# Attention of a hybrid block on one core: scores and meta values from stacked high and low rows, in another order

## The chip, the core and the metric

The kernel runs on one core of a Trainium2 chip. Its engines run side by side and meet at semaphores: PE (TensorE, matmuls into PSUM; PEld is its loading of weights), DVE (VectorE), ACT (ScalarE), POOL (GpSimd) and SP, which issues transfers. The metric is the device time of one execution in microseconds (us), as the median of the runs. Times inside the kernel are from one execution that the hardware profiler took; they count from the start of its span.

## The reference, cut to what matters

One decoder block over 16 meta tokens and 512 tokens: an HGRN2 recurrence and a sliding-window attention side by side, merged by sigmoid gates, then a PEER expert layer. The change lies in the attention:

```
s_band = einsum(q, k of the token's block and of the block before) * scale    # masked to a window of 128
s_meta = einsum(q, k of the 16 meta tokens) * scale
p = softmax(concatenate([s_band, s_meta, sink of the head]))
o = einsum(p_band, v) + einsum(p_meta, v of the meta tokens)
```

There are 8 query heads of 64 dimensions, in two groups with one key and value head each (`s` = 0 and 1 in the code), and 4 blocks of 128 tokens. Float32 accuracy is wanted. A product of float32 values is formed either as one float32 matmul, or from parts: a high part rounded to the matmul's short format (`F32R`) and a low part that holds the rest.

## The kernel before, in words

**Stages.** Input projections (to about 130 us), the recurrence with its chunks of 32 tokens (to 181 us), the attention (181 to 275 us), the branch and output projections, the queries and keys of the expert layer, and from 549 us on the dense and gathered products over the experts. The code of each engine is written out by hand in program order, and semaphores tie the engines together. `S["anorm"]` and its like are those semaphores: `wait_ge` stops an engine until the count is reached.

**The attention** has 16 steps (`HEADS`), one for a pair of heads (one of each group) in one block of tokens: step `p` is block `tt = p // 4`, pair `c = p % 4`. For each:
- PE `scores(p)` (L1823, in the first block L1827 and L1829): two float32 matmuls over 64 rows each, one for a group, with the query as weights and the keys `akx` as 272 moving columns (256 of the band, 16 meta; 144 in the first block).
- DVE `logits(p)`: copies the sink into the last column (L1244), scales and masks (L1245), takes the maximum (L1248).
- ACT `exponentials(p)` (L810), twice, with the row sum.
- DVE `normalise(p)`: reciprocal (L1255), two scalings of `atp` (L1257), the meta part into `atpm` (L1258).
- PE `turn(p)` (L1845, L1846): four transposes (two in the first block) and one of the meta part.
- ACT `turned(p)` (L818, L819): copies what was transposed out of PSUM.
- PE `values(p)` (L1859, L1862, L1865): float32 matmuls of 128 columns, in pairs for the two groups: band before, own band, meta.

When a block of tokens is done, ACT takes its high part (`attention_hi`, L823) and DVE the low part (`attention_lo`, L1264).

**What fills PE in between.** `gate_products` (L1709) are 256 matmuls of 512 columns of the gate projection (and 8 ahead of them), dealt out over the 17 rounds of the loop over `i` by `gates_before`: 15 or 16 in a round. Twenty-four of them use one tile of weights. When those are done, ACT copies the result (L768) and makes the high part of the next tile (L706), POOL makes its low part (L555, 128x1024 elements) and scales the gates (L566). A round is, on PE, `scores(i)`, `turn(i - 1)`, the gate products, `values(i - 1)`. DVE and ACT also split the output of the recurrence (`ohg`, L1280 and L840) in four rounds.

**Ahead of it** DVE builds `avm` and `akx` at about 104 us, while PE still projects, and PE transposes twelve groups of values and keys at 131 us (`avmeta` last). In the experts' part `middle_and_low` (L1416) splits gate values into three bf16 parts.

## Time and profile before

| what | us |
|---|---|
| median of 3 runs (1569.6 to 1570.4) | 1569.93 |
| the profiled execution itself | 1569.61 |
| its span | 1567.9 |
| PE busy, whole span | 1561.1 |
| attention, first scores to first branch product (181.18 to 275.35) | 94.17 |
| PE / DVE / ACT / POOL busy, 181.00 to 275.35 | 94.30 / 53.30 / 50.72 / 39.98 |

A busy time counts overlapping instructions once. A matmul's duration runs from its start to the modelled end, while the next one begins before that; how much of PE's time a matmul takes is therefore read from one start to the next, or from the pieces of the chain of waits, which don't overlap. A duration on DVE or ACT that is far longer than that of the same instruction elsewhere has a wait inside it.

### The profile page before, as it was taken

What the parts mean: (1) busy time and instruction counts of PE and PEld (TensorE: products, weight loads), DVE (VectorE), ACT (ScalarE), POOL (GpSimd) and SP (SyncE); (2) the same over time, 40 slices, a digit from 0 to 9 for tenths busy, and PEclk for the clock granted to TensorE, in tenths of its full rate; (3) what the DMA queues carried; (4) which work ended last, traced back from release to release, by engine and by line L of the source; (5) the groups of instructions that cost most, each with busy time, mean ns of one, the idle gap of its engine ahead of it and who ended that gap; (6) DMA issues with size and microseconds to landing.
All of it is one profiled execution on the core that took longest, in us unless ns stands there. A gap on an engine that the chain in (4) does not pass through costs nothing.

```text
span 1567.9 us, 26041 instructions
## 1 busy us (share of the span) xinstructions
PE 1561.1 (100%) x9638; PEld 1385.4 (88%) x9638; DVE 1250.8 (80%) x2495; ACT 688.6 (44%) x1008; POOL 753.8 (48%) x484
## 2 busy tenths in 40 slices
PE   9999999999999999999999999999999999999998
PEld 9987777888889999999999999898989899888887
DVE  5864565745899899999598888787888888888887
ACT  6323355534434367777434333333333333333334
POOL 4674443434557566654165555455545545322220
PEclk9999999999999999999999999999999999999999
DMA  4222122434223479998899998999999989899994
GB/s 164 94 94 68 56 67 68 150 121 146 82 81 124 121 261 304 341 321 277 310 366 358 334 353 332 354 340 346 338 348 339 367 319 351 296 320 322 330 321 148
DMA packets 151731, 385.45 MB, mean 246 GB/s; under 512 B 11872, under 2 KB 61536, under 8 KB 151520
## 3 DMA queue, kind: packets, MB, share of 16 engines
...
## 4 chain that ended last, share of the span: by engine, by line
PE 89%; DVE 10%; DMA 0%; ACT 0%; issue 0%; SPq 0%
PE ps L2146 31%; PE ps L1989 25%; PE ps L1646 6%; PE ps L1709 6%; PE ps L2007 5%; DVE hot_w L1530 3%; PE ps L1895 3%; DVE rows L1469 2%; PE ps L1608 2%; DVE hot_l L1526 1%; DVE hot_l L1531 1%; DVE hot_l L1527 1%; PE ps L1908 1%; PE ps L2132 1%; PE ps L1654 1%; PE ps L2070 1%
## 5 line engine op out<-in xcount | busy, mean ns | idle before, releaser
L1989 PE MATMUL ps<-hThi,uwhi 128*128 128x352 f32 x1024 | 330.1, 326 | 0.0
L1989 PE MATMUL ps<-hTlo,uwhi 128*128 128x352 f32 x1024 | 327.6, 322 | 0.0
L956 ACT ACTIVATE vwhi<-vraw 128x1024 fp32r<-128x1024 f32 x128 | 135.8, 1061 | 407.9 <-PE ps L2146 349.6
L653 POOL DMA_INDIRECT rows<-in_v,gidx x128 | 164.4, 1284 | 249.9 <-DVE acc L1485 233.6
L653 POOL DMA_INDIRECT rows<-in_u,gidx x128 | 189.8, 1483 | 181.1 <-DVE rows L1478 136.2
L1444 DVE TENSOR_TENSOR vwlo<-vraw,vwhi 128x1024 fp32r<-128x1024 f32 x128 | 156.6, 1223 | 114.5 <-ACT vwhi L956 114.2
L910 ACT ACTIVATE uwhi<-uraw 128x1024 fp32r<-128x1024 f32 x127 | 134.4, 1058 | 169.6 <-PE ps L1989 130.8
L1989 PEld LDWEIGHTS ps<-hTlo,uwhi 128*128 128x128 f32 x1024 | 192.6, 188 | 1.6
L1989 PEld LDWEIGHTS ps<-hThi,uwhi 128*128 128x128 f32 x1024 | 192.2, 188 | 1.9 <-issue 0.3
L1989 PE MATMUL ps<-hThi,uwlo 128*128 128x352 f32 x1024 | 183.8, 322 | 0.0
L2146 PE MATMUL ps<-vwhi,awhi 128*128 128x512 f32 x720 | 183.7, 390 | 0.0
L2146 PE MATMUL ps<-vwlo,awhi 128*128 128x512 f32 x720 | 182.7, 389 | 0.0
L2146 PE MATMUL ps<-vwhi,awlo 128*128 128x512 f32 x720 | 182.7, 389 | 0.0
L613 POOL TENSOR_TENSOR uwlo<-uraw,uwhi 128x1024 fp32r<-128x1024 f32 x52 | 125.5, 2414 | 95.4 <-ACT uwhi L910 53.5
L1485 DVE SCALAR_TENSOR_TENSOR acc<-rows,pick_w,acc 128x1024 f32<-128x1024 f32 x128 | 164.4, 1285 | 3.7 <-DMA rows<-in_v,gidx 1.1
L1989 PEld LDWEIGHTS ps<-hThi,uwlo 128*128 128x128 f32 x1024 | 166.7, 188 | 0.0
L2146 PEld LDWEIGHTS ps<-vwlo,awhi 128*128 128x128 f32 x720 | 135.1, 188 | 28.3
L2146 PEld LDWEIGHTS ps<-vwhi,awlo 128*128 128x128 f32 x720 | 135.1, 188 | 28.1
L1478 DVE SCALAR_TENSOR_TENSOR rows<-rows,ynat 128x1024 f32<-128x1024 f32 x128 | 155.0, 1232 | 4.0 <-DMA rows<-in_u,gidx 3.9
L2146 PEld LDWEIGHTS ps<-vwhi,awhi 128*128 128x128 f32 x720 | 134.0, 188 | 25.7
L555 POOL TENSOR_TENSOR wzlo<-raw,wzhi 128x1024 fp32r<-128x1024 f32 x35 | 86.0, 2457 | 121.7 <-ACT wzhi L706 121.7
L551 POOL TENSOR_TENSOR wlo<-raw,whi 128x1024 fp32r<-128x1024 f32 x28 | 67.2, 2401 | 88.0 <-ACT whi L704 88.0
...
## 6 DMA issues: line engine op xcount, KB each, us to landing
vraw<-in_v SPq DMA_DIRECT2D x128, 512.0 KB, 5.2
...
rows<-in_u,gidx POOLq DMA_INDIRECT x128, 7.4
```

The source lines that it names most:

```text
L555: pool.tensor_tensor(spaced(k, "lo"), loaded(k), spaced(k, "hi").bitcast(F32), ALU.subtract).then_inc(S["w_lo"], 1)
L613: pool.tensor_tensor(u_weights("lo", n, False), uraw[:, n % 2, :], u_weights("hi", n, False).bitcast(F32), ALU.subtract).then_inc(S["u_lo" ...
L653: pool.indirect_dma_start(out=rows[n % SLOTS][:], out_offset=None, in_=u if q < P else v, in_offset=bass.IndirectOffsetOnAxis(ap=gidx[:, q ...
L910: act.activation(u_weights("hi", n, n >= LAG), u_raw(n, k), ACT.Copy).then_inc(S["u_hi"], 1)
L956: act.activation(vw["hi"][:, m % 2, :], vraw[:, m % 2, :], ACT.Copy).then_inc(S["v_hi"], 1)
L1444: dve.tensor_tensor(vw["lo"][:, m % 2, :], vraw[:, m % 2, :], vw["hi"][:, m % 2, :].bitcast(F32), ALU.subtract).then_inc(S["v_lo"], 1)
L1478: dve.scalar_tensor_tensor(out=row[:], in0=row[:], scalar=1.0, in1=ynat[:, 0, :], op0=ALU.mult, op1=ALU.mult, accum_out=dots[:, k:k + 1]). ...
L1485: dve.scalar_tensor_tensor(out=acc[:, 0, :], in0=row[:], scalar=pick_w[:, k:k + 1], in1=acc[:, 0, :], op0=ALU.mult, op1=ALU.add).then_inc( ...
L1646: ins = pe.matmul(dst, z_weights(k, a, c), y[b][:, SLOT[c], own], start=i == 0, stop=i == 3 * DC - 1)
L1709: ins = pe.matmul(ps[:, 2 + t % 2, :], z_weights(t % 2, a, c), y[b][:, SLOT[c], META:LEN], start=i % (3 * DC) == 0, stop=(i + 1) % (3 * DC ...
L1989: ins = pe.matmul(ps[:, k, 0:UCOLS], u_weights(a, k, far)[:, c * P:(c + 1) * P], hT[b][:, c, P + EXTRA:TOK], start=i == 0, stop=i == len(U ...
L2146: ins = pe.matmul(ps[:, 2 + j, :], act_w[a][:, k, j // 2 * P:(j // 2 + 1) * P], vw[b][:, k, j % 2 * 512:(j % 2 + 1) * 512], start=first an ...
```

## The change

Names: `CUR` is 144, a block of keys with the 16 meta keys in front of it.

- **Scores.** The keys are split once into `key_hi` and `key_lo`, each stacked twice in the 128 partitions (64 dimensions, and the same again). The queries of a block are split into `query`, with the high part in 64 partitions and the low part in the other 64. A head's scores are then two matmuls over 128 rows, against the high and the low keys, in the short format. `queries(tt, s)` is new work for DVE: block 0 in the chunk loop, the others in rounds 1, 2, 4, 6, 8 and 10.
- **Order on PE.** `scores(i + 1)` stands in the middle of round `i`'s gate products, `turn(i - 1)` ahead of them; the last `turn_outputs` also moves between gate products.
- **Meta values.** `avmeta` and `atpTm` hold high and low rows in all combinations (4 x 32 rows). ACT writes the high rows of `atpTm` twice, DVE the low rows (`meta_lo`, new). `turn(p)` now also waits for `meta_lo(p - 1)`.
- **Values** are formed for four pairs at once, in 512 columns, once in each block of tokens, in rounds 4, 8, 12 and 16.
- **Sinks** are copied once for all pairs, since `atsc` now has four places.
- **ACT** does `exponentials(i)` ahead of `turned(i - 1)`, DVE `normalise(i)` ahead of `attention_lo`.
- `middle_and_low` has one operation fewer, POOL two memsets fewer.

```diff
+CUR = P + META
+KEY_ROW = (TOK // P) * CUR
...
+QUERIES = {1: (1, 0), 2: (1, 1), 4: (2, 0), 6: (2, 1), 8: (3, 0), 10: (3, 1)}
...
+def low_count(p):
+
+    return min(2 * p + 3, 2 * HEADS)
...
-        avmeta = at("avmeta", [P, P], F32, X + 30144)
-        akx = at("akx", [P, TT - 1, KEYS], F32, X + 22784)
+        avmeta = at("avmeta", [P, P], F32R, X + 30144)
+        avm4 = at("avm4", [P, 2, 2, 2 * META], F32R, X + 30656)
+        key_hi = at("key_hi", [P, 2, KEY_ROW], F32R, Y_END + HH * LEN * 4)
+        key_lo = [at("key_lo0", [P, KEY_ROW], F32R, Y_END + HH * LEN * 4 + 8 * KEY_ROW),
+                  at("key_lo1", [P, KEY_ROW], F32R, X + 22784)]
+        query = at("query", [P, 2, 2, 4, P], F32R, Z + Z_META * LEN * 4)
...
-        atsc = at("atsc", [P, 2, KEYS + 8], F32, X)
-        atp = at("atp", [P, 2, KEYS + 8], F32, X + 2240)
-        atpT = at("atpT", [P, 2, BAND], F32, X + 4480)
-        atpTm = at("atpTm", [P, P], F32, X + 30656)
+        atsc = at("atsc", [P, 4, 2, 2 * CUR], F32, X)
+        atp = at("atp", [P, 2, 2 * CUR], F32, X + 64 * CUR)
+        atpT = at("atpT", [P, 4, 2, BAND], F32, X + 80 * CUR)
+        atpTm = at("atpTm", [P, 4, P], F32R, Z + 8 * LEN * 4)
...
-            pool.memset(avmeta[:], 0.0)
-            pool.memset(atpTm[:], 0.0)
...
-                    act.activation(atp[:, s, lo:KEYS + 1], atsc[:, s, lo:KEYS + 1], ACT.Exp, bias=atstat[:, 0, s:s + 1],
+                    act.activation(atp[:, s, lo:KEYS + 1], atsc[:, p % 4, s, lo:KEYS + 1], ACT.Exp, bias=atstat[:, 0, s:s + 1],
...
             def turned(p):
 
                 lo = P if p < 4 else 0
                 act.wait_ge(S["atr_mm"], p + 1)
-                need(act, S["apv_mm"], p)
-                act.activation(atpT[:, :, lo:BAND], ps[:, 4:6, lo:BAND], ACT.Copy).then_inc(S["atr_out"], 1)
-                act.activation(atpTm[0:2 * META, :], ps[0:2 * META, 4, BAND:BAND + P], ACT.Copy).then_inc(S["atr_out"], 1)
+                c = p % 4
+                need(act, S["apv_mm"], p // 4)
+                act.activation(atpT[:, c, :, lo:BAND], ps[:, 4:6, lo:BAND], ACT.Copy).then_inc(S["atr_out"], 1)
+                for at_row in (0, 4 * META):
+                    ins = act.activation(atpTm[at_row:at_row + 2 * META, c, :], ps[0:2 * META, 4, BAND:BAND + P], ACT.Copy)
+                ins.then_inc(S["atr_out"], 1)
...
             for i in range(HEADS + 1):
                 if i >= 5 and i % 4 == 1:
                     attention_hi(i // 4 - 1)
+                if i < HEADS:
+                    exponentials(i)
                 if i:
                     turned(i - 1)
-                if i < HEADS:
-                    exponentials(i)
...
-            ins.then_inc(S["avm_ok"], 1)
-            for i in range(TT - 1):
-                dve.tensor_copy(akx[:, i, 0:BAND], ak_z[:, META + i * P:META + i * P + BAND])
-            dve.tensor_copy(akx[:, :, BAND:KEYS], ak_z[:, 0:META].unsqueeze(1).to_broadcast([P, TT - 1, META])
-                            ).then_inc(S["akx_ok"], 1)
+            chain.done(ins)
+            both = avm[:].unsqueeze(1).to_broadcast([P, 2, 2 * META])
+            chain.done(dve.tensor_copy(avm4[:, 0], both))
+            dve.tensor_tensor(avm4[:, 1], both, avm4[:, 0].bitcast(F32), ALU.subtract).then_inc(S["avm_ok"], 1)
+            tiles = lambda ap: ap.rearrange("p (i x) -> p i x", x=CUR)
+            rows_of = [slice(s * HD, (s + 1) * HD) for s in range(2)]
+            for s, kv in enumerate(rows_of):
+                own = ak_z[kv, META:LEN].rearrange("p (i x) -> p i x", x=P)
+                first = ak_z[kv, 0:META].unsqueeze(1).to_broadcast([HD, TT, META])
+                for rows_ in rows_of:
+                    dve.tensor_copy(tiles(key_hi[rows_, s])[:, :, META:CUR], own)
+                    ins = dve.tensor_copy(tiles(key_hi[rows_, s])[:, :, 0:META], first)
+                chain.done(ins)
+                high = tiles(key_hi[kv, s].bitcast(F32))
+                for rows_ in rows_of:
+                    dve.tensor_tensor(tiles(key_lo[s][rows_])[:, :, META:CUR], own, high[:, :, META:CUR], ALU.subtract)
+                    ins = dve.tensor_tensor(tiles(key_lo[s][rows_])[:, :, 0:META], first, high[:, :, 0:META], ALU.subtract)
+            ins.then_inc(S["qk_ok"], 1)
...
+            def queries(tt, s):
+
+                kv, other = rows_of[s], rows_of[1 - s]
+                raw_q = aq_z[kv, :, tt * P:(tt + 1) * P]
+                chain.done(dve.tensor_copy(query[kv, tt % 2, s], raw_q))
+                dve.tensor_tensor(query[other, tt % 2, s], raw_q, query[kv, tt % 2, s].bitcast(F32), ALU.subtract
+                                  ).then_inc(S["qk_ok"], 1)
...
+                if c == NCH - 2:
+                    dve.wait_ge(S["z_out"], N_Z)
+                    for s in range(2):
+                        queries(0, s)
...
-                dve.tensor_copy(atsc[:, :, KEYS:KEYS + 1], sink[:].rearrange("p (s c) -> p s c", s=2)[:, :, c:c + 1])
-                chain.done(dve.scalar_tensor_tensor(out=atsc[:, :, lo:KEYS], in0=ps[:, 6:8, lo:KEYS], scalar=HD ** -0.5,
+                if p == 0:
+                    dve.tensor_copy(atsc[:, :, :, KEYS], sink[:].rearrange("p (s c) -> p c s", s=2))
+                chain.done(dve.scalar_tensor_tensor(out=atsc[:, c, :, lo:KEYS], in0=ps[:, 6:8, lo:KEYS], scalar=HD ** -0.5,
...
             def normalise(p):
@@ -1254,9 +1293,19 @@
                 dve.wait_ge(S["aexp"], 2 * (p + 1))
                 chain.done(dve.reciprocal(atstat[:, 2, :], atstat[:, 1, :]))
                 for s in range(2):
-                    dve.tensor_scalar(atp[:, s, lo:BAND], atp[:, s, lo:BAND], atstat[:, 2, s:s + 1], None, ALU.mult)
-                dve.tensor_tensor(atpm[:], atp[:, :, BAND:KEYS], atstat[:, 2, :].unsqueeze(2).to_broadcast([P, 2, META]),
+                    own = atp[:, s, :].rearrange("p (b x) -> p b x", x=CUR)[:, lo // P:2, 0:P]
+                    dve.tensor_scalar(own, own, atstat[:, 2, s:s + 1], None, ALU.mult)
+                dve.tensor_tensor(atpm[:], atp[:, :, P:CUR], atstat[:, 2, :].unsqueeze(2).to_broadcast([P, 2, META]),
                                   ALU.mult).then_inc(S["anorm"], 1)
+
+            def meta_lo(p):
+
+                c, rows_m = p % 4, slice(0, 2 * META)
+                dve.wait_ge(S["atr_out"], 2 * (p + 1))
+                for at_row in (2 * META, 6 * META):
+                    ins = dve.tensor_tensor(atpTm[at_row:at_row + 2 * META, c, :], ps[rows_m, 4, BAND:BAND + P],
+                                            atpTm[rows_m, c, :].bitcast(F32), ALU.subtract)
+                ins.then_inc(S["anorm"], 1)
...
+                normalise(i)
+                if i:
+                    meta_lo(i - 1)
                 if i >= 5 and i % 4 == 1:
                     attention_lo(i // 4 - 1)
-
-                normalise(i)
+                if i in QUERIES:
+                    queries(*QUERIES[i])
                 if i >= HD_AT + 1 and (i - HD_AT) % 2 == 1 and i < HD_AT + 1 + 2 * HH:
                     h = (i - HD_AT) // 2
                     dve.wait_ge(S["ohg_hi"], h + 1)
                     dve.tensor_tensor(ohg["lo"][:, h, :], o_hg[:, h, :], ohg["hi"][:, h, :].bitcast(F32),
                                       ALU.subtract).then_inc(S["ohg_ok"], 1)
+            meta_lo(HEADS - 1)
...
-                chain.done(dve.tensor_tensor(rest, rest, tab[:, 1], ALU.subtract))
-                return dve.tensor_copy(tab[:, 2], rest)
+                return dve.tensor_tensor(tab[:, 2], rest, tab[:, 1], ALU.subtract)
...
-                    srcs = [v_z[:, h, 0:META] for h in range(HH)] if n == 10 else [avm[:]]
-                rows = P if n < 9 else META if n < 11 else 2 * META
+                    srcs = ([v_z[:, h, 0:META] for h in range(HH)] if n == 10 else
+                            [avm4[:].rearrange("p a b m -> p (a b m)").bitcast(F32)])
+                rows = META if 9 <= n < 11 else P
...
-                halves = [slice(s * HD, (s + 1) * HD) for s in range(2)]
-                if tt:
-                    for s, kv in enumerate(halves):
-                        ins = pe.matmul(ps[:, 6 + s, 0:KEYS], aq_z[kv, c, tt * P:(tt + 1) * P], akx[kv, tt - 1, :],
-                                        start=True, stop=True)
-                else:
-                    for s, kv in enumerate(halves):
-                        pe.matmul(ps[:, 6 + s, P:BAND], aq_z[kv, c, 0:P], ak_z[kv, META:META + P], start=True, stop=True)
-                    for s, kv in enumerate(halves):
-                        ins = pe.matmul(ps[:, 6 + s, BAND:KEYS], aq_z[kv, c, 0:P], ak_z[kv, 0:META], start=True, stop=True)
+                pe.wait_ge(S["qk_ok"], 1 + 2 * (tt + 1))
+                lo, first = (0, META + (tt - 1) * CUR) if tt else (P, 0)
+                last = first + KEYS - lo
+                for s in range(2):
+                    pe.matmul(ps[:, 6 + s, lo:KEYS], query[:, tt % 2, s, c, :], key_hi[:, s, first:last], start=True, stop=False)
+                    ins = pe.matmul(ps[:, 6 + s, lo:KEYS], query[:, tt % 2, s, c, :], key_lo[s][:, first:last],
+                                    start=False, stop=True)
                 ins.then_inc(S["asc_mm"], 1)
...
-            pe.wait_ge(S["akx_ok"], 1)
             scores(0)
             gate_products(GATES_TURN + TT * GATES_HG, GATES_TURN + TT * GATES_HG + GATES_MID)
-            turn_outputs(TT - 1)
-
...
             def turn(p):
 
-                pe.wait_ge(S["anorm"], p + 1)
+                pe.wait_ge(S["anorm"], low_count(p - 1) if p else 1)
                 need(pe, S["atr_out"], 2 * p)
                 for s in range(2):
                     for q in range(0 if p >= 4 else 1, 2):
-                        pe.transpose(ps[:, 4 + s, q * P:(q + 1) * P], atp[:, s, q * P:(q + 1) * P], ident[:])
...
-            def values(p):
-
-                tt, c = p // 4, p % 4
-                pe.wait_ge(S["atr_out"], 2 * (p + 1))
-                if c == 0:
-                    need(pe, S["oat_ok"], tt - 1)
+            def values(tt):
+
+                pe.wait_ge(S["atr_out"], 8 * (tt + 1))
+                need(pe, S["oat_ok"], tt - 1)
+                if tt == 0:
                     pe.wait_ge(S["ohg_f"], TT)
+                pe.wait_ge(S["anorm"], low_count(4 * tt + 3))
+                pe.matmul(ps[:, tt % 2, :], avmeta[:], atpTm[:].rearrange("p c t -> p (c t)"), start=True, stop=False)
                 heads = [(s, slice(s * HD, (s + 1) * HD)) for s in range(2)]
-                if tt:
+                for block_, own in ((tt - 1, slice(0, P)), (tt, slice(P, BAND))):
+                    if block_ < 0:
+                        continue
                     for s, kv in heads:
-                        pe.matmul(ps[kv, tt % 2, c * P:(c + 1) * P], avnat[:, tt - 1, kv], atpT[:, s, 0:P],
-                                  start=True, stop=False)
-                for s, kv in heads:
-                    pe.matmul(ps[kv, tt % 2, c * P:(c + 1) * P], avnat[:, tt, kv], atpT[:, s, P:BAND],
-                              start=tt == 0, stop=False)
-                for s, kv in heads:
-                    ins = pe.matmul(ps[kv, tt % 2, c * P:(c + 1) * P], avmeta[:, kv], atpTm[:], start=False, stop=True)
+                        ins = pe.matmul(ps[kv, tt % 2, :], avnat[:, block_, kv], atpT[:, :, s, own], start=False, stop=block_ == tt)
                 ins.then_inc(S["apv_mm"], 1)
 
             for i in range(HEADS + 1):
-                if 1 <= i < HEADS:
-                    scores(i)
                 if i:
                     turn(i - 1)
-                gate_products(gates_before(i), gates_before(i + 1))
-                if i:
-                    values(i - 1)
+                first, last = gates_before(i), gates_before(i + 1)
+                gate_products(first, (first + last) // 2)
+                if i == 0:
+                    turn_outputs(TT - 1)
+                if i + 1 < HEADS:
+                    scores(i + 1)
+                gate_products((first + last) // 2, last)
+                if i and i % 4 == 0:
+                    values(i // 4 - 1)
```

PE, rounds 4 and 5 before, from the last gate product of one round to the first of the next (L1709 are the gate products, L1823 the scores, L1845 and L1846 the turn, the others the values):

```order
L1709 MATMUL ps<-yhi,wzhi 128x512
L1862 MATMUL ps<-atpT,avnat 64x128 x2
L1865 MATMUL ps<-atpTm,avmeta 64x128 x2
L1823 MATMUL ps<-akx,zr 128x272 x2
L1845 MATMUL ps<-ident,atp 128x128 x4
L1846 MATMUL ps<-ident,atpm 32x128
L1709 MATMUL ps<-ylo,wzhi 128x512
```

The same place with the change, in the round that has the values of the first block (L1761 are the gate products, L1877 and L1878 the scores, L1903 and L1909 the values, L1892 and L1893 the turn):

```order
L1761 MATMUL ps<-ylo,wzhi 128x512
L1877 MATMUL ps<-key_hi,query 128x272
L1878 MATMUL ps<-key_lo_86,query 128x272
L1877 MATMUL ps<-key_hi,query 128x272
L1878 MATMUL ps<-key_lo_87,query 128x272
L1761 MATMUL ps<-yhi,wzlo 128x512
...
L1761 MATMUL ps<-yhi,wzhi 128x512
L1903 MATMUL ps<-atpTm,avmeta 128x512
L1909 MATMUL ps<-atpT,avnat 64x512 x2
L1892 MATMUL ps<-ident,atp 128x128 x4
L1893 MATMUL ps<-ident,atpm 32x128
```

The scores have moved ahead of half of the gate products, and the values stand in one place for four steps.

DVE before, one step of the attention, in a round with a part of `ohg`:

```order
L1244 COPY atsc<-sink 128x2
L1245 SCALAR_TENSOR_TENSOR atsc<-ps,bandmask 128x2x272
L1248 TENSOR_REDUCE atstat<-atsc 128x2
L1255 RECIPROCAL atstat<-atstat 128x2
L1257 TENSOR_SCALAR atp<-atp,atstat 128x256 x2
L1258 TENSOR_TENSOR atpm<-atp,atstat 128x32
L1280 TENSOR_TENSOR ohglo<-o_hg,ohghi 128x512
```

DVE with the change, round 8, in which the first group's queries of block 3 are split (L1306 is `meta_lo`, L1211 and L1212 `queries`):

```order
L1284 SCALAR_TENSOR_TENSOR atsc<-ps,bandmask 128x2x272
L1287 TENSOR_REDUCE atstat<-atsc 128x2
L1294 RECIPROCAL atstat<-atstat 128x2
L1297 TENSOR_SCALAR atp<-atp,atstat 128x2x128 x2
L1298 TENSOR_TENSOR atpm<-atp,atstat 128x32
L1306 TENSOR_TENSOR atpTm<-ps,atpTm 32x128 x2
L1211 CAST query<-zr 64x512
L1212 TENSOR_TENSOR query<-zr,query 64x512
L1284 SCALAR_TENSOR_TENSOR atsc<-ps,bandmask 128x2x272
```

The copy of the sink is gone, and `meta_lo` and `queries` stand between one step's normalising and the next step's logits.

## Rows read from the trace of the kernel before

**Rows 1.** The page, parts 1 and 4: busy time by engine, shares of the chain

```profile
PE 1561.1 (100%) x9638; PEld 1385.4 (88%) x9638; DVE 1250.8 (80%) x2495; ACT 688.6 (44%) x1008; POOL 753.8 (48%) x484
PE 89%; DVE 10%; DMA 0%; ACT 0%; issue 0%; SPq 0%
```

**Rows 2.** Windows, attention: us, busy by engine, clock, DMA share, GB/s

```profile
181.00:275.35 94.35, 94.30 (x605) 70.58 (x597) 53.30 (x122) 50.72 (x135) 39.98 (x22) 1.00 0.20 62
```

**Rows 3.** Chain of waits in the attention: start us, us, engine, line

```profile
181.18 0.42 PE ps L1827 x4
...
225.23 0.37 PE ps L1859 x4
225.60 0.22 PE ps L1862 x4
...
226.04 0.66 PE ps L1823 x4
...
227.39 3.44 PE ps L1709 x15
...
233.00 3.71 PE ps L1709 x16
...
253.18 1.13 ACT atp L810 x4
...
275.35 43.75 PE ps L1895 x192
```

**Rows 4.** PE timeline, short-format matmuls of 264, 256 and 128 columns: start us, us

```profile
27.92 2.10 PE L1654 MATMUL ps<-yhi,wzlo 128*128 128x264 f32 x16
...
390.69 0.22 PE L2021 MATMUL ps<-keyparts,q2lo 128*128 128x128 f32 x1
...
390.92 0.22 PE L2021 MATMUL ps<-keyparts,q2lo 128*128 128x128 f32 x1
```

**Rows 5.** PE timeline, four transposes among gate products

```profile
178.61 0.60 PE L1789 MATMUL ps<-ident,o_nat 128*128 128x128 f32 x4
178.97 0.48 PE L1709 MATMUL ps<-yhi,wzhi 128*128 128x512 f32 x1
179.28 0.39 PE L1709 MATMUL ps<-ylo,wzhi 128*128 128x512 f32 x1
```

**Rows 6.** DVE timeline, one step: start us, us, [idle before <-releaser]

```profile
249.66 2.10 DVE L1244 COPY atsc<-sink 128x2 f32<-128x2 f32 x1 [1.35 <-PE ps L1823]
251.68 0.71 DVE L1245 SCALAR_TENSOR_TENSOR atsc<-ps,bandmask 128x544 f32<-128x544 f32 x1
252.42 0.72 DVE L1248 TENSOR_REDUCE atstat<-atsc 128x2 f32<-128x546 f32 x1
254.33 0.17 DVE L1255 RECIPROCAL atstat<-atstat 128x2 f32<-128x2 f32 x1 [1.19 <-ACT atp L810]
254.53 0.61 DVE L1257 TENSOR_SCALAR atp<-atp,atstat 128x256 f32<-128x256 f32 x2
255.07 0.18 DVE L1258 TENSOR_TENSOR atpm<-atp,atstat 128x32 f32<-128x32 f32 x1
```

**Rows 7.** POOL timeline beside that step

```profile
249.35 2.39 POOL L555 TENSOR_TENSOR wzlo<-raw,wzhi 128x1024 fp32r<-128x1024 f32 x1 [3.30 <-ACT wzhi L706]
```

**Rows 8.** Groups by line, 181.00 to 275.35: busy us, mean ns, idle before, releaser

```profile
L1244 DVE COPY atsc<-sink 128x2 f32<-128x2 f32 x16 | 13.0, 813 | 19.3 <-PE ps L1823 12.6 <-PE ps L1829 6.4
L566 POOL TENSOR_TENSOR gates<-gates,rstd 128x512 f32 (+1 forms) x11 | 14.3, 1300 | 0.0
L706 ACT ACTIVATE wzhi<-raw 128x1024 fp32r<-128x1024 f32 x10 | 10.5, 1047 | 0.0
L1280 DVE TENSOR_TENSOR ohglo<-o_hg,ohghi 128x512 fp32r<-128x512 f32 x4 | 2.7, 685 | 0.0
```

**Rows 9.** DVE timeline, an operation with two SBUF inputs, before the attention

```profile
99.92 2.90 DVE L1166 TENSOR_TENSOR qi<-zr,ecol 128x512 f32<-128x512 f32 x1
```

**Rows 10.** Waits, 0 to 300 us: engine, line, releaser, us in total, times, longest

```profile
DVE vnat L1183 <- PE ps L1733: 27.1, 2, 26.0
```

**Rows 11.** DVE timeline, end of the recurrence's states

```profile
175.90 1.11 DVE L1221 SCALAR_TENSOR_TENSOR state<-state,ecol,ps 128x128 f32<-128x128 f32 x4
```

11 lines of the change are left out of this document (6 added, 5 removed).

## The prediction

> **What bounds the kernel now.** First the page: PE is busy 1561.1 of 1567.9 us and holds 89% of the chain that ended last, DVE 10% [rows 1]. The change lies in the attention, so next that stretch alone: PE is busy throughout at full clock, DVE for 53.3 and ACT for 50.7 of 94.35 us [rows 2]. The chain of waits goes through PE from 181.18 to the first branch product at 275.35, 94.17 us [rows 3]. So the attention is bound by PE's work, and what PE loses in work is gained as long as nothing else becomes late. A low busy share of DVE and ACT doesn't say that they have time: their steps hang on one another, and the last question is how long one step's ring through them is.
>
> **PE's work before.** Sixteen gate products take 3.71 us of the chain and fifteen 3.44, 0.230 each, so the 264 of this stretch take 60.7. The rest is 94.2 - 60.7 = 33.5. A late round agrees: 227.39 to 233.00 is 5.61, less 3.44, leaves 2.17, of which the scores are 0.66, the first pair of values 0.37 and a further pair 0.22 [rows 3].
>
> **PE's work after, by part.**
> - Scores: four matmuls in the short format over all 128 rows. Sixteen of 264 columns took 2.10 - 0.16 = 1.94 from start to next start, 0.12 each; a 256 and a 128 column one together took 0.23, so a narrow one about 0.11 [rows 4]. With 272 columns I take 0.125, so 0.50 a step where 0.66 stood; with 144 columns 0.115, so 0.46. Above, 0.17 each if every weight load showed (0.23 less half of a narrow one's 0.12). Sum: 12 x 0.50 + 4 x 0.46 = 7.8.
> - Turn: four transposes between gate products take 0.36, and the gate product behind them starts 0.08 late (0.31 where 0.23 is usual) [rows 5]. With a fifth at 0.11: 0.55, and 0.37 in the first block. Sum: 12 x 0.55 + 4 x 0.37 = 8.1.
> - Values: 128 columns of a pair took 0.22, so 512 columns take 0.88, as four before; one pair in the first block, two in the three others, each time with one meta matmul at 0.23 and 0.15 for getting in (0.37 - 0.22) [rows 3]. Sum: 7 x 0.88 + 4 x 0.38 = 7.7. The gain is here: the meta pairs of sixteen steps shrink to four matmuls. Above, 0.19 more for a pair if the wide float32 ones went at the rate of the scores' (0.66 for 272 columns, 1.07 less 0.88 allowing for their fixed part), 1.3 in all.
> - The last turn of the recurrence: 0.44.
>
> Together 24.0. PE saves **9.5 us**, between 6 and 10.5.
>
> **The ring through DVE and ACT.** In program order DVE now does logits, normalise, `meta_lo`, and, in many rounds, something more, before it comes to the next logits; ACT's exponentials stand between the first two. Before, DVE had waited 1.35 for the next scores at this place [rows 6], so nothing hung on its length. Now the ring runs by itself, since the scores come half a round ahead. One turn of it, from [rows 3] and [rows 6]: scaling to the exponentials' start 253.18 - 251.68 = 1.50; exponentials until the reciprocal 1.15; reciprocal and scalings 0.74; `atpm` 0.10 until the next can start; `meta_lo` two small operations. The trace has none of these. Below it is 0.10 each, above half of the 0.71 that 544 columns from PSUM take; I take 0.23, nearer to the 0.18 of the one of 32 columns. Sum **3.95**. It is longer by
> - `queries`, 64x512 copied and subtracted. Two scalings of 256 took 0.54, so 0.46 with its wait for 512; a subtraction of that width takes 0.685 [rows 8] and 0.60 if another follows. I take 1.06; above, 1.35.
> - `ohg`'s low part and `attention_lo`, 0.60 each.
>
> Rounds 4 to 10 hold queries four times, `ohg` three times and `attention_lo` twice: 7 x 3.95 + 4 x 1.06 + 5 x 0.60 = 34.9. PE in those rounds: 7 x (0.50 + 0.55) + 108.5 x 0.230 + 1.26 + 2.14 of values = 35.7. Even without a further wait the two are level.
>
> **The further wait is POOL.** The sink's copy of two elements lasted 2.10, until the end of POOL's 2.39 [rows 6, 7]; the sixteen averaged 0.813 [rows 8] where 0.17 would do. An operation with two SBUF inputs lasted 2.90 in the same way [rows 9] where 0.685 is usual. The sinks' copies are gone and with them about 10 us of such waits, but those lay beside PE's work. What remains takes their place, now inside the ring: the scalings in every round, both operations of `queries`, `ohg`'s low part. POOL holds 2.39 + 1.30 for each 24 gate products, 7.7 us at 5.0 for a round of 15.5: a place that meets it at random waits (2.39 x 2.39 + 1.30 x 1.30) / 2 / 7.7 = 0.48. Rounds 4 to 10 have 7 scalings, 4 queries and 3 `ohg`: 14 x 0.48 = 6.7. The ring is then 41.6, and PE waits **5.9**.
>
> Outside those rounds: the first scalings stand behind the recurrence's last turn, which is moved to later, and behind POOL, while PE comes to `turn(0)` sooner, 0.5. Rounds 1 to 3 have a ring of 3.1 and 4.1 with queries against PE's 4.4, about even, 0.2. Rounds 11 to 14 have a ring of 3.95 + 0.48 against 4.6 to 6.7, covered. In round 15 no scores are left and PE has 3.5 us of gate products, while a tile of weights ends at the close of round 14, so that ACT's copy and split (0.5 and 1.05 [rows 8]), the exponentials and then POOL's two operations come in one row: about 1.5. PE waits 5.9 + 0.5 + 0.2 + 1.5 = **8.1**, between 2 and 13.
>
> **Trace and notes.** These holds are in the rows above. The Trainium skill, SBUF — State Buffer, section "Who interferes with whom", says that the second of the two engines fully blocks when DVE runs a two-port mode or reads two SBUF inputs; by that the PSUM-reading `meta_lo` and logits go free and both operations of `queries` can be held, which leaves the sum as it is, while a reader who took only copies for exposed would leave out three places, 1.4 us. A rule that speaks against the change: TensorEngine Tiling (Array Packing), section "Overview", promises up to twice the speed for two groups of at most 64 rows side by side, which stacking to 128 rows gives up. The 0.66 for the two float32 scores [rows 3] is above the 0.50 expected for the stacked ones, so the sum keeps the rows.
>
> **Costs at nothing.** The keys' split is 16 operations on DVE at about 104 us, some 5 us where 1 stood; DVE then waited 26.0 us for PE's first transposes [rows 10]. Block 0's queries, 2.1 us and one hold of at most 1.3, start when the last state is done at 177.0 [rows 11] and PE wants them at 181.1. If that cover fell short by the hold, 0.5. The operation less in `middle_and_low` and POOL's memsets lie on no chain that I can see. Behind the attention PE goes on without a gap [rows 3], and all that follows is released by PE and DVE, so a shift is kept.
>
> **Sum.** The profiled execution took 1569.61, its span 1567.9. 1569.61 - 9.5 + 8.1 = 1568.2; the median is 0.3 above that execution: **1568.5**.
>
> **Rivals.**
> 1. Holds meet the ring seldom: POOL's operations follow ACT's split in a fixed beat, and the sink copies' mean excess was 0.64 a step, so they could as well fall while DVE waits for the exponentials. With 2 to 4 us of waits: 1562.4 to 1564.4. For it speaks that DVE idles for 1.15 in each turn of the ring.
> 2. The ring wins altogether, slower than before. Its place is `turn(p)` behind `meta_lo(p - 1)`, its price the excess of 14 to 16 rounds over PE's 5.2 on average. From a ring of 5.8 on average, with holds, the saving is gone; at 6.1, which a scaling that loses its speed on the now spaced rows (0.27 more each) would bring, PE waits 14 us: 1574.4. Against it, rounds 11 to 14 have little extra.
> 3. Queries, holds and stacks cost as said, but the wide values go slower (1.3) and the scores too (2.2): of these 3.5 about half only fills waits that are there already, so 1.7 shows: 1570.2.
> 4. The attention gets shorter and the gain is given back later, by a wait that a shift changes (DVE holds 10% of the chain [rows 1]): 1569.9. Nothing in the trace asks for it.
>
> **How the numbers follow.** Forecast 0.45 (1566 to 1571), rival 1 0.25, rival 2 0.12, rival 3 0.12, rival 4 0.06. The range leaves out the lowest and highest tenth: 1562.8 to 1573. A measurement of this kernel can tell about 0.2%, 3.1 us, from no change, so faster means under 1566.8: rival 1 and a little of the forecast, 0.30. Slower means above 1573.1: most of rival 2 and a little more, 0.12. The same: 0.58.
>
> **What would show it.** Right: first scores to first branch product takes 91 to 94 us, with 24 us beside the gate products and visible waits of PE, most of them in rounds 4 to 10 for DVE's `meta_lo` (turn) or its logits (scores), and one ahead of the last turn; scalings and queries on DVE with durations up to 2.4 us that end with POOL's. Each step's prices: scores 0.50, turn 0.55, values 1.26 and 2.14. Wrong: the stretch at 85 to 88 us with no PE waits (rival 1), or over 97 (rival 2), or a stretch that is shorter while the end isn't (rival 4).

## The result, and the profile after

| | before | after |
|---|---|---|
| median, us | 1570.22 | 1574.88 |
| ratio, 95% interval | | 1.003 (1.0021 to 1.0038) |
| span of the profiled execution | 1567.9 | 1572.3 |
| first scores to first branch product | 94.1 | 96.2 |
| first branch product to the end of the span | 1292.6 | 1294.5 |

The change makes the kernel slower by 4.7 us, 0.3%. The forecast of 1568.5 and its range (to 1573.0) both miss. The spans differ by 4.4 to 4.5: 0.5 is there when the first scores start, nearly all of it from the kernel's beginning (the second transfer of the input took 4.66 us and not 4.23), 2.1 arise in the attention, and 1.9 behind it. The other 0.2 or so lies between medians and profiled executions.

The page, parts 1 and 4, against [rows 1]:

```profile
PE 1557.5 (99%) x9478; PEld 1380.7 (88%) x9478; DVE 1279.9 (81%) x2540; ACT 691.9 (44%) x1024; POOL 754.3 (48%) x482
PE 83%; DVE 13%; issue 1%; ACT 1%; DMA 0%; POOL 0%; ACTq 0%; SPq 0%; DVEq 0%
```

PE held 89% of the chain that ended last and now holds 83%. The windows of the attention (us, then busy us and instructions of PE, PEld, DVE, ACT, POOL, the granted clock, DMA share, GB/s), after in the first row, against [rows 2]:

```profile
181.68:277.85 96.17, 89.23 (x437) 65.39 (x437) 67.48 (x151) 54.18 (x151) 42.02 (x22) 1.00 0.18 61
```

PE is no longer busy throughout: 7 us are idle in which the clock stays full, and DVE works 67.5 us where 53.3 stood. The list of waits, same stretch, engine PE (what waited, for what, us in total, times, longest):

```profile
PE ps L1892 <- DVE atpTm L1306: 3.8, 4, 1.9
PE ps L1903 <- DVE atpTm L1306: 2.0, 3, 1.1
PE ps L1877 <- DVE atstat L1287: 0.3, 1, 0.3
PE ps L1892 <- DVE atpm L1298: 0.3, 1, 0.3
```

L1892 is the turn, L1903 the first values, L1306 `meta_lo`. PE waits for DVE's low rows, at the place that rival 2 named; the longest of these waits, 1.9, is the one for the last turn. The chain of waits of rounds 7 and 8 (start us, us, engine, line):

```profile
220.92 0.74 DVE atsc L1284
221.68 0.73 DVE atstat L1287
...
222.87 0.70 ACT atp L820 x3
223.59 0.18 DVE atstat L1294
223.79 0.61 DVE atp L1297 x2
224.41 0.10 DVE atpm L1298
224.54 0.28 DVE atpTm L1306
224.84 0.28 DVE atpTm L1306
...
225.15 0.69 DVE ohglo L1332
225.84 0.64 DVE atsc L1284
226.51 0.73 DVE atstat L1287
...
228.62 1.57 DVE atp L1297 x2
...
230.93 0.43 DVE query L1211
231.38 0.04 DVE query L1212
231.42 2.74 issue
234.15 0.73 DVE atsc L1284
```

The chain doesn't touch PE from 186 to 255 us. One turn is logits (0.74, 0.73), exponentials (1.15), reciprocal, scalings (0.61), `atpm`, `meta_lo` (0.28 twice), then an extra, then the next logits. Round 7 with `ohg`'s low part is 4.9 long, round 8 is 8.3: its scalings last 1.57 and the second operation of `queries` 2.74 where 0.69 is usual. They stand while POOL works, whose rows of the same stretch are:

```profile
226.11 2.41 POOL L565 TENSOR_TENSOR wzlo<-raw,wzhi 128x1024 fp32r<-128x1024 f32 x1 [7.52 <-ACT wzhi L716]
228.47 1.30 POOL L576 TENSOR_TENSOR gates<-gates,rstd 128x512 f32 x1
230.94 2.63 POOL L565 TENSOR_TENSOR wzlo<-raw,wzhi 128x1024 fp32r<-128x1024 f32 x1 [1.17 <-ACT wzhi L716]
```

### The profile page after: what moved, and what is told of

It is laid out like the page before. It is cut to its first block, busy times and chain, and to the rows that moved or that the text cites. A ratio compares the mean times of both kernels' runs of the same rounds, so it can differ in the third digit from the quotient of the medians.

```text
span 1572.3 us, 25792 instructions
## 1 busy us (share of the span) xinstructions
PE 1557.5 (99%) x9478; PEld 1380.7 (88%) x9478; DVE 1279.9 (81%) x2540; ACT 691.9 (44%) x1024; POOL 754.3 (48%) x482
## 4 chain that ended last, share of the span: by engine, by line
PE 83%; DVE 13%; issue 1%; ACT 1%; DMA 0%; POOL 0%; ACTq 0%; SPq 0%; DVEq 0%
PE ps L2194 31%; PE ps L2037 25%; PE ps L1698 6%; PE ps L2055 5%; DVE hot_w L1582 3%; PE ps L1943 3%; PE ps L1761 3%; DVE rows L1521 2%; DVE hot_l L1578 1%; DVE hot_l L1583 1%; DVE hot_l L1579 1%; PE ps L1956 1%; PE ps L2180 1%; PE ps L1706 1%; PE ps L2118 1%
## 5 line engine op out<-in xcount | busy, mean ns | idle before, releaser
L663 POOL DMA_INDIRECT rows<-in_u,gidx x128 | 186.4, 1456 | 185.4 <-DVE rows L1530 143.2
L2194 PE MATMUL ps<-vwhi,awhi 128*128 128x512 f32 x720 | 183.8, 390 | 0.0
L561 POOL TENSOR_TENSOR wlo<-raw,whi 128x1024 fp32r<-128x1024 f32 x28 | 67.2, 2400 | 88.3 <-ACT whi L714 88.3
```

The costliest lines, as they stand in the source:

```text
L663: pool.indirect_dma_start(out=rows[n % SLOTS][:], out_offset=None, in_=u if q < P else v, in_offset=bass.IndirectOffsetOnAxis(ap=gidx[:, q ...
L2194: ins = pe.matmul(ps[:, 2 + j, :], act_w[a][:, k, j // 2 * P:(j // 2 + 1) * P], vw[b][:, k, j % 2 * 512:(j % 2 + 1) * 512], start=first an ...
```

## The experiments

Fifteen kernels, each timed against the kernel before, whose median was 1570.0 to 1570.5 from one set of runs to the next; a ratio is to that of its own set. The edits are cut to what matters. "Stretch" is first scores to first branch product and "tail" the rest of the span, both from the profile; the clock column says whether a window of 5 us in or just behind the attention had a granted clock under 1.00.

| kernel | median us | ratio to before | stretch | tail | clock fell |
|---|---|---|---|---|---|
| before | 1570.2 | 1 | 94.1 | 1292.6 | no |
| changed | 1574.9 | 1.0030 | 96.2 | 1294.5 | no |
| e1 extras under the exponentials | 1573.5 | 1.0022 | 96.6 | 1294.1 | yes |
| e2 meta_lo later | 1583.5 | 1.0082 | 105.7 | 1295.0 | yes |
| e3 queries twice | 1587.6 | 1.0108 | 110.4 | 1294.9 | yes |
| e4 small low part | 1567.8 | 0.9982 | 90.3 | 1294.2 | yes |
| e5 ACT scales | 1566.4 | 0.9976 | 88.3 | 1294.4 | no |
| e6 last round | 1571.8 | 1.0013 | 94.1 | 1294.6 | no |
| e7 all of e5, e1 and e6 | 1567.6 | 0.9984 | 90.1 | 1294.9 | no |
| e8 float32 scores | 1573.7 | 1.0022 | 96.5 | 1293.9 | yes |
| e9 before, one operation fewer | 1570.0 | 0.9999 | 94.1 | 1292.6 | no |
| e10 extras ahead of meta_lo | 1570.5 | 1.0003 | 93.5 | 1295.4 | yes |
| e11 and atpm on ACT | 1570.0 | 1.0000 | 91.4 | 1295.1 | no |
| e12 changed, operation back | 1574.7 | 1.0029 | 97.4 | 1295.6 | no |
| e13 before, shifted | 1573.3 | 1.0018 | 97.0 | 1293.8 | no |
| e14 before, key split | 1569.9 | 0.9998 | 94.1 | 1292.8 | no |
| e15 ACT scales, last round | 1565.4 | 0.9969 | 87.7 | 1293.4 | no |

The intervals are 0.1 to 0.15% to either side. The stretch of e13 has its twelve added matmuls in it. e12 has the changed kernel's attention and a stretch 1.2 longer: how POOL and the ring meet differs that much between executions, so a difference of 1 us between two stretches proves nothing.

### What makes the ring long: e1, e3, e4

**e4** leaves the order alone and takes POOL's operation away:

```diff
-spread_lo(it * 2 + (k + 2), k)              # POOL, wzlo, 2 x 512 columns
+pool.tensor_tensor(some(spaced(k, "lo")), ...)   # the same, 2 x 16 columns
```

> The changed kernel in which POOL makes only 16 of 512 columns of the low part of the gate weights from the fifth tile on (part of the low weights is left out of the computation), so that its 2.39 us operation is nearly gone from the attention; its scaling of the gates, 1.3 us, stays. Theory A with the holds as small as the trace of the changed kernel shows them (about 7 us in all on DVE, of which 3 to 4 in rounds where the ring is the longer one): stretch 92 to 94, time 1571 to 1573. Theory B (holds decide): stretch 90 to 91, time 1569 to 1570. Theory C: no change.

Measured 1567.8, 7.1 us faster than the changed kernel and beyond what either theory gave; the stretch fell by 5.9, although the clock fell once in it. The groups of DVE in the attention, changed kernel (line, operation, count, busy us, mean ns):

```profile
L1297 DVE TENSOR_SCALAR atp<-atp,atstat 128x256 f32<-128x256 f32 x24 | 13.8, 614 | 0.4
L1212 DVE TENSOR_TENSOR query<-zr,query 64x512 fp32r<-64x512 f32 x6 | 6.2, 1029 | 0.2
L1297 DVE TENSOR_SCALAR atp<-atp,atstat 128x128 f32<-128x128 f32 x8 | 5.1, 674 | 0.1
```

and e4:

```profile
L1304 DVE TENSOR_SCALAR atp<-atp,atstat 128x256 f32<-128x256 f32 x24 | 9.4, 435 | 0.4
L1219 DVE TENSOR_TENSOR query<-zr,query 64x512 fp32r<-64x512 f32 x6 | 4.1, 686 | 0.2
L1304 DVE TENSOR_SCALAR atp<-atp,atstat 128x128 f32<-128x128 f32 x8 | 1.9, 284 | 0.1
```

The same operations are 9.7 us shorter in all. Nothing but POOL's operation was made smaller, so this is what POOL held them for. The rows of the logits and of `meta_lo`, which read PSUM, are equal in both (722 and 282 ns).

**e1** takes the extras out from behind `meta_lo`:

```diff
 logits(i)
+# attention_lo (one round later), queries, ohg's low part
 normalise(i)
 meta_lo(i - 1)
-# attention_lo, queries, ohg's low part
```

> The changed kernel with another order on DVE: queries, the low part of ohg and attention_lo stand between a round's logits and its normalise, where DVE otherwise idles 1.15 us for the exponentials (attention_lo one round later than before). Theory A (the attention waits for the ring through DVE and ACT, 4.2 us bare and 5.4 to 6.0 with these extras): the ring falls to about 4.3 in every round, below PE's 5.2 on average, so nearly all of the 6.9 us in which PE idled between 181 and 278 us goes: stretch 96.2 -> 90 to 92, time 1569 to 1571. Theory B (not the extras but POOL's holds on DVE's operations make the ring too long): at most 1 to 2 us, 1573 to 1574, since the scalings stay exposed. Theory C (PE's own work is dearer than thought): no change, 1575.

Measured 1573.5, by the number theory B. But the stretch is not shorter (96.6), and two things ate what the empty place under the exponentials gave. First the holds, since POOL's low part follows ACT's split and ACT's split stands just ahead of the exponentials, so POOL works in that very place:

```profile
L1297 DVE TENSOR_SCALAR atp<-atp,atstat 128x256 f32<-128x256 f32 x24 | 14.4, 640 | 0.4
L1211 DVE CAST query<-zr 64x512 fp32r<-64x512 f32 x6 | 7.1, 1190 | 0.1
L1212 DVE TENSOR_TENSOR query<-zr,query 64x512 fp32r<-64x512 f32 x6 | 7.0, 1174 | 0.2
L1329 DVE TENSOR_TENSOR ohglo<-o_hg,ohghi 128x512 fp32r<-128x512 f32 x4 | 6.7, 1685 | 0.0
```

With e4's rows as the undisturbed ones, the holds are some 18 us, twice as much. Second, PE's clock. Windows of e1:

```profile
216.00:221.00 5.00, 2.96 (x16) 2.28 (x15) 4.79 (x10) 1.13 (x4) 1.89 (x2) 0.96 0.31 105
221.00:226.00 5.00, 5.00 (x19) 3.98 (x18) 3.75 (x10) 3.56 (x9) 0.78 (x1) 0.70 0.00 0
...
271.00:276.00 5.00, 4.33 (x14) 3.32 (x14) 1.14 (x5) 1.01 (x3) 0.00 (x0) 0.66 0.27 93
```

PE was busy for 3 of 5 us, and then the granted clock was 0.70 on average; from 220.7 to 224.0 alone it was 0.50, the lower of the two levels (1.2 GHz), and eight gate products took 3.37 us where 1.85 is usual. A window at 0.70 costs 1.5 us and one at 0.66 up to 1.7, so e1 lost an estimated 3 us to the clock. The two causes weren't tried apart.

**e3** puts 1.17 more into four rounds:

```diff
+if i in (4, 6, 8, 10):
+    queries_again(*QUERIES[i])
 if i in QUERIES:
     queries(*QUERIES[i])
```

> The changed kernel in which DVE splits the queries twice in rounds 4, 6, 8 and 10, 1.17 us more in each of these four rounds; nothing else differs. Theory A (ring): every added us shows, 4 x 1.17 = 4.7, so 1579.6. Theory B (holds by POOL decide): the added operations only shift where the holds fall, 0 to 3, 1575 to 1578. Theory C (PE's work): no change, 1575.

Measured 1587.6: 12.7 slower than the changed kernel, not 4.7. All theories were too small. The added 4.7 stand there; the operations of `queries` were held for 9 us where the changed kernel has 2; and six windows have clocks of 0.70 to 0.96, an estimated 5 us of PE's work. Three of them:

```profile
211.00:216.00 5.00, 2.21 (x9) 1.70 (x8) 3.68 (x7) 1.75 (x6) 1.15 (x1) 0.79 0.28 105
256.00:261.00 5.00, 3.39 (x11) 2.80 (x12) 3.63 (x10) 2.04 (x8) 0.00 (x0) 0.72 0.21 86
286.00:291.00 5.00, 5.00 (x19) 3.13 (x17) 0.56 (x2) 1.01 (x3) 0.00 (x0) 0.70 0.02 10
```

So a us in the ring can cost more than a us.

### What takes the holds out of it: e2, e5, e7

**e2** has e1's order and moves `meta_lo` away from the turn, by a float32 copy of the turned rows in SBUF, which is also one more operation for ACT in each step:

```diff
+act.activation(atraw[0:2 * META, c, :], ps[0:2 * META, 4, BAND:BAND + P], ACT.Copy)
...
-dve.tensor_tensor(atpTm[...], ps[rows_m, 4, BAND:BAND + P], atpTm[rows_m, c, :], ALU.subtract)
+dve.tensor_tensor(atpTm[...], atraw[rows_m, c, :], atpTm[rows_m, c, :], ALU.subtract)
```

> As e1_under_exp, and meta_lo is taken out of the ring: ACT also copies the turned meta rows as float32 into SBUF, so that DVE makes the low rows one round later, between logits and normalise, and turn(p) waits only for normalise(p) and ACT's copies. Theory A: the ring falls by another 0.6 us, to 3.6 us, below PE's 4.4 in the first rounds too: stretch 89 to 91, time 1568 to 1570, the fastest of these. Theory B: 1 us better than e1 at most, 1572 to 1573. If meta_lo, which now reads two SBUF inputs, is held by POOL, up to 0.5 of a round is given back.

Measured 1583.5, the opposite. The operation has the same size, but both inputs are now in SBUF, and the group tells the rest:

```profile
L1325 DVE TENSOR_TENSOR atpTm<-atraw,atpTm 32x128 fp32r<-32x128 f32 x32 | 22.3, 697 | 2.1 <-ACT atpTm L850 1.5
```

282 ns became 697, 13.3 us of holds in all: 23 of the 32 still took 0.28, and nine took 1.3 to 2.5. The clock fell twice as well, at waits of PE of 4 and 5 us, an estimated 4.7 us lost; e2 doesn't tell how much of its 10.0 over e1 comes from each of these. One of the holds on DVE's timeline, and POOL's row beside it:

```profile
258.92 2.83 DVE L1325 TENSOR_TENSOR atpTm<-atraw,atpTm 32x128 fp32r<-32x128 f32 x2
...
259.19 2.40 POOL L583 TENSOR_TENSOR wzlo<-raw,wzhi 128x1024 fp32r<-128x1024 f32 x1 [2.21 <-ACT wzhi L734]
```

The first of the pair ran, the second stood until POOL was done. The Trainium skill, SBUF — State Buffer, section "Who interferes with whom", says that an operation of DVE with at most one SBUF input, outside its two-port modes, doesn't contend with GpSimd, and that one with two does when GpSimd reads SBUF; these rows agree, 282 ns for each of the 32 with one SBUF input against a mean of 697 with two.

**e5** leaves the order and lets ACT scale:

```diff
+def scaled(p):          # ACT, behind turned(p - 1)
+    act.activation(own, own, ACT.Copy, scale=atstat[:, 2, s:s + 1])
...
-    dve.tensor_scalar(own, own, atstat[:, 2, s:s + 1], None, ALU.mult)
```

> The changed kernel in which ACT, not DVE, multiplies the probabilities by the reciprocal (two copies with a scale, after turned(i - 1)); DVE keeps the reciprocal, atpm and meta_lo and can go on to the next logits. Nothing is left out. The runs so far say that POOL's two SBUF operations hold DVE's SBUF operations (10.1 us of holds in the changed kernel, 7.7 of them on the scalings; 21.1 with the other order; 2.3 with POOL's low part nearly gone, when the stretch fell from 96.2 to 90.3). Theory B (holds inside the ring decide): 7.7 us of holds and 0.5 of a ring are gone, ACT's 54 us of 96 rise to about 65, PE hardly waits until the last turn: stretch 96.2 -> 88 to 90, time 1566 to 1569. Rival (the bare length of the ring and ACT's share of it decide): ACT's scalings, 0.35 each, take the place of DVE's 0.31, so the ring keeps its length and only some waits move: 1572 to 1575.

Measured 1566.4, as theory B said; faster than before by 0.24% (0.14 to 0.33). ACT's scalings and what DVE has left to hold:

```profile
L829 ACT ACTIVATE atp<-atp,atstat 128x256 f32<-128x256 f32 x24 | 10.9, 502 | 0.3
...
L1306 DVE TENSOR_TENSOR atpm<-atp,atstat 128x32 f32<-128x32 f32 x16 | 8.8, 548 | 0.5
```

```profile
181.51:269.79 88.28, 86.74 (x436) 66.09 (x436) 54.73 (x119) 66.65 (x183) 40.15 (x22) 1.00 0.21 66
```

The scaling on ACT is slower than DVE's undisturbed one (0.50, not 0.30) and still better: POOL doesn't hold it, and DVE goes on to `meta_lo` meanwhile. `atpm` takes over as the held one (548 ns for 182).

**e7** combines e5, e1's order and e6.

> The changed kernel with ACT's scaling, the last exponentials ahead of the split, and queries, ohg's low part and attention_lo between logits and normalise on DVE. Theory B: only queries and ohg's low part can still be held by POOL, and they are no longer behind one another with the scalings; PE waits under 3 us in all, stretch 86 to 88, time 1564 to 1567, faster than both kernels by 0.2 to 0.4%. Rival: as with the order alone, the holds only move (21.1 instead of 10.1), onto the reciprocal that ACT now waits for: 1569 to 1572.

Measured 1567.6, between the two expectations and no better than e5. The rival's mechanism is in the trace, if smaller: `ohg`'s low part and `queries` lasted up to 2.5 and 2.9 us ahead of the reciprocal that ACT waits for.

### The rest of the attention: e6, e8, e10, e11, e15

**e6** does the last exponentials ahead of the gate tile's copy and split. **e15** is the same on e5.

```diff
-for t in gate_blocks_done(gates_before(i), gates_before(i + 1)):
+# ACT: the tile that ends in round 14 is copied and split in round 15, behind exponentials(15)
```

> The changed kernel in which ACT, in the last rounds, does the last exponentials ahead of the copy and the split of the gate tile that ends in round 14, not behind them. In the changed kernel PE waits from 266.8 to 273.0 us for its last turn: ACT's 0.47 copy and 0.9 split stand ahead of the exponentials, and then POOL's 2.40 us holds the scaling for 2.0. If that wait is what it seems: exponentials 1.4 earlier, scaling not held, wait 6.2 -> 2.5 to 3, time 1571 to 1572. Rival: the weights of the first branch tile, whose split is now 2.5 later, are then late in their place and PE waits for them: 1574 to 1576.

> The kernel in which ACT scales (1566.4), and the last exponentials stand ahead of the copy and the split of the gate tile of round 14. PE's last wait there was 0.6, its exponentials stood 1.4 behind ACT's copy and split. Expected: 0.6 gained at the last turn, but the branch tile is split 2.5 later and its low part ends at about 270, when the first branch product is due: 1565.5 to 1567.

e6 measured 1571.8, as expected, and in the place foretold: PE's wait for the last turn is gone and the stretch 2.1 shorter. The time is 3.1 lower; 1 us of that is not from there, and is within the intervals. Part of the agreement is luck, for that wait was 1.9 us, not 6.2: I had taken the length of the side chain through ACT and DVE for PE's wait; the row that counts is PE's own:

```profile
273.00 0.66 PE L1892 MATMUL ps<-ident,atp 128*128 128x128 f32 x4 [1.89 <-DVE atpTm L1306]
```

e15 measured 1565.4, the lowest of all, 0.31% under before (0.18 to 0.43); its interval overlaps e5's, so the step from e5 isn't shown by the times.

**e8** leaves the scores in float32 and drops `queries` and the split of the keys:

```diff
-pe.matmul(ps[...], query[:, tt % 2, s, c, :], key_hi[:, s, first:last], start=True, stop=False)
-pe.matmul(ps[...], query[:, tt % 2, s, c, :], key_lo[s][:, first:last], start=False, stop=True)
+pe.matmul(ps[...], aq_z[kv, c, tt * P:(tt + 1) * P], key_f[kv, first:last], start=True, stop=True)
```

> The changed kernel with the scores left as float32 products over 64 rows, from the raw queries and one float32 copy of the keys; no queries, no split of the keys. Values, meta rows, sinks and the order stay as changed. PE's scores cost 0.66 in place of 0.50 in twelve rounds: +1.9. The ring is shorter by 1.16 in six rounds and by one hold of 2.05. If the ring decides: 4 x 1.16 + 2.05 in rounds 4 to 10 less 1.1 for PE, so the stretch falls by about 3 to 5: 1570 to 1572. If PE's work decided: +1.9, 1576.5 to 1577.

Measured 1573.7, between the two. PE's scores cost 1.3 more (9.7 against 8.4, from start to start), the 1.2 of `queries` is gone from six rounds, and yet the stretch is 96.5: the scalings now meet POOL more often (busy 15.6 and 5.8 where 13.8 and 5.1 stood), and the clock fell once. The stacked scores by themselves, with the splits that they need, are worth about nothing here. No run takes the wide values or the new order on PE back alone.

**e10** and **e11** start from e5 with the extras between `normalise(i)` and `meta_lo(i - 1)`; both also have `middle_and_low` as before, which e9 and e12 below show to be worth nothing; e11 gives `atpm` to ACT as well.

> The kernel in which ACT scales (1566.4), with queries, attention_lo and ohg's low part between normalise(i) and meta_lo(i - 1) on DVE, and middle_and_low as before. In its trace meta_lo(i - 1) waits 0.9 us for ACT's copies of the turned rows, and the ring of rounds 4 to 10 is still 4.9 to 5.5 long. If 0.9 of each extra hides there, the stretch falls from 88.4 to 86.5 to 87.5; with theory D another 1.8 less: 1563 to 1565. Rival: POOL's holds move onto the extras, as in the first order tried, and nothing is gained: 1566 to 1567.

> As e10_extras_first, and ACT also makes atpm (two copies of 16 columns, about 0.15 each), so that of DVE's operations in the ring only queries, ohg's low part and attention_lo are left for POOL to hold. The 5.7 us of holds on atpm go, ACT gets about 5 us more work. Expected: stretch 86 to 87, 1562.5 to 1564.5; if ACT's longer row of copies matters more, 0.5 to 1.5 slower than e10_extras_first.

Measured 1570.5 and 1570.0: both expectations wrong, by some 6 us. The order of e5 had the extras where they delay only the next logits, whose scores come half a round early. Ahead of `meta_lo` they delay the turn itself. The chain of e10:

```profile
226.74 1.27 DVE atpm L1306
228.01 1.50 DVE query L1221
...
229.57 0.68 issue
230.25 0.28 DVE atpTm L1314
230.54 0.30 DVE atpTm L1314
...
230.97 0.62 PE ps L1913
231.58 3.36 PE ps L1919 x8
```

Two holds, then `meta_lo`, and PE's values then take 3.36 in place of 1.87, with a granted clock of 0.66 in that window.

### The tail: e9, e12, e13, e14

Behind the attention the code differs in one operation only.

```diff
-chain.done(dve.tensor_tensor(rest, rest, tab[:, 1], ALU.subtract))
-return dve.tensor_copy(tab[:, 2], rest)
+return dve.tensor_tensor(tab[:, 2], rest, tab[:, 1], ALU.subtract)
```

> The kernel before with nothing but the one operation fewer in middle_and_low. From the first branch product to the end of the span the kernel before took 1292.6 us and all nine kernels with the change 1293.9 to 1295.0 (mean 1294.4), whether their attention ended 5.6 us earlier or 16.1 later. So the 1.8 us given back later do not depend on the shift. Theory D: the missing operation moves the beat of DVE against POOL in the part that DVE bounds; then 1571 to 1572. Rival: something else of the change, or the noise of single profiles: 1570.0.

> The changed kernel with middle_and_low as before. Theory D: the tail falls from 1294.4 to 1292.6, time 1573.1. Rival: 1574.9.

1570.0 and 1574.7: theory D, that this operation explains the longer tail, falls twice. e14 adds the split of the keys to the kernel before, e13 twelve matmuls ahead of the branch:

> The kernel before with the sixteen operations that split the keys added on DVE at about 104 us, their results unused, under the 26.0 us in which DVE waits there. My prediction had them at nothing. Expected by it: 1570.2. If they cost something in the recurrence or behind it (theory F would have it here): up to 1572.

> The kernel before with twelve matmuls of 512 columns into an unused PSUM bank between the attention and the first branch product, 12 x 0.23 = 2.8 us. Tail means first branch product to the end of the span: 1292.6 in the kernel before, 1294.1 to 1295.6 in ten of the changed kernels, 1293.9 with float32 scores. Theory E (any shift of that stage costs 1.5 to 2 us in the part that DVE, POOL and the transfers share): 1570.2 + 2.8 + 1.8 = 1574.8, tail 1294.4. Theory F (the tail hangs on something in the changed code, not on the shift): 1573.0, tail 1292.6.

e14 measured 1569.9: the split is free, as predicted. e13 measured 1573.3, 2.9 more for 2.8 of work, which speaks for theory F, but its profile has a tail of 1293.8, two thirds of the way to theory E. Against a mere shift speaks e6: its first branch product starts at 275.30, as before (275.28), and its tail is 2.0 longer. So neither theory holds as it stands. One profile's tail is no surer than 1 us (e12, the changed kernel but for an operation that costs nothing, has 1.1 more); but the thirteen kernels with the change have 1293.4 to 1295.6, and the three without it and without a shift 1292.6 to 1292.8.

Laid side by side, the traces of before and changed part at three places above all: 0.3 between 480 and 520 us, 1.1 between 700 and 730, 0.3 near 1530. At the second DVE is the bound (busy for 183.8 of the 185 us from 555 to 740), and its 32 products with the gathered rows, 45.3 us in all before, take 47.2. One of them makes the difference. Before, with POOL's row behind it:

```profile
711.77 1.21 DVE L1469 SCALAR_TENSOR_TENSOR rows<-rows,ynat_x 128x1024 f32<-128x1024 f32 x1
713.00 2.41 POOL L613 TENSOR_TENSOR uwlo<-uraw,uwhi 128x1024 fp32r<-128x1024 f32 x1 [4.62 <-DVE rows L1469]
```

and after:

```profile
714.42 2.40 POOL L623 TENSOR_TENSOR uwlo<-uraw,uwhi 128x1024 fp32r<-128x1024 f32 x1 [3.06 <-ACT uwhi L923]
714.75 3.16 DVE L1521 SCALAR_TENSOR_TENSOR rows<-rows,ynat_x 128x1024 f32<-128x1024 f32 x1
```

POOL now starts 0.33 ahead of DVE, DVE stands until it is done, and at 720.97 PE waits 0.92 for DVE's `hot_l`, where it went on before. The same hold stands in e5 (3.10) and e6 (3.14), with a wait of PE of 1.0 in each; e13 has one of 3.38 at another place and waits of 0.6 and 0.5. So most of the 1.9 is one more hold. What makes POOL and DVE meet there in each of these kernels stays open.

## Why the prediction was wrong, point by point

- **What bounds the attention**: right for before. The warning that the last question is the ring's length was the right one.
- **PE saves 9.5 (6 to 10.5)**: mis-sized by about 1.4. The prices in the rows were right (scores 0.50; values 1.01 and 1.87, behind 0.23 to 0.47 for the meta matmul). But e5, which has hardly a wait, still needs 88.3; without its three waits on DVE (1.5 idle, and 0.17 each hidden by the end of the matmul ahead) and some short delays it is about 86. So PE saves about 8.1.
- **The bare ring, 3.95**: 4.23 in the rows: `meta_lo` 0.28 an operation (0.23 taken), `atpm` until `meta_lo` 0.13 to 0.22 (0.10), a row of semaphores between them. `queries` 1.17 (1.06).
- **Holds of 6.7 in rounds 4 to 10**: 4.0. From the logits of round 4 (203.8) to those of round 11 (245.0) the seven rounds took 41.2, where the sum had 34.9 + 6.7 = 41.6: that was luck, by two errors, 2.3 too little of ring and 2.7 too much of holds. PE's waits come to the 5.9 predicted (3.9 idle in the timeline and 0.17 hidden in each of eleven), but only 4.2 of them are waits for DVE's rounds 4 to 10. The other 1.7 stand in rounds 11 and 12, at 246.5, 249.6 and 255.1, which the prediction called covered: the ring was still late there.
- **Outside those rounds**: `turn(0)` 0.5, right. Rounds 1 to 3: 0.2 predicted, 0.9 at `turn(3)` (203.1); their ring was 5.0 on average with two held scalings. Last turn: 1.5 predicted, 2.1, by the mechanism given (ACT's copy and split, exponentials, POOL). The remaining 0.8 or so is many small delays that the sum had not: behind a wait the first matmul of the scores takes 0.23 until the next starts, not 0.12.
- **Sum of the attention: the step that failed.** Predicted -9.5 + 8.1 = -1.4; it was about -8.1 + 10.2 = +2.1, so 3.5 of the 6.4 us between forecast and measurement arose here, and with them the sign. The mechanism was right, PE's saving against a ring with holds in it; the terms that were mis-sized are PE's saving (1.4), the waits of rounds 1 to 3 (0.7), the last turn (0.6) and the small delays (0.8), each on the kind side.
- **"All that follows ... so a shift is kept": the second step that failed.** 1.9 us came on top, 1.1 of them at one hold of DVE by POOL near 715 us. Without them the time would be 1573.0, at the edge of the range; with the attention alone as predicted it would be about 1571. The last 1 us of the miss is the 0.5 ahead of the attention and the 0.8 (0.3 taken) by which the median is above the profiled execution; nothing in the change is known to cause it.
- **Rival 2 (1574.4, 0.12)** had place and sign. Its number was met by luck: it had 4.5 from the attention, which gave 2.1, and the tail gave most of the rest. Its cause, a scaling that loses its speed on spaced rows, didn't occur: two wide scalings took 0.61 where 0.54 stood. Its sign "over 97" wasn't seen either: 96.2.
- **Rival 4 (0.06)** wanted a shorter attention, which didn't come; but something was given back later, and with e5 and e15, whose attention is shorter, the tail is longer too (1294.4 and 1293.4 for 1292.6).
- **Rival 1** rested on DVE's idle 1.15 in each turn of the ring. e1 and e7 show that POOL works there too.
- **Costs at nothing**: the key split (e14) and the operation in `middle_and_low` (e9), right. Block 0's queries too: from the last products of the recurrence to the first scores it is 0.57 before and 0.58 after. POOL's memsets were not tried alone.
- **What would show it**: waits of PE for `meta_lo` and logits, scalings and queries that end with POOL's: seen. "91 to 94 us" for the stretch: not.
